# A decoder layer in split float32: gate and up products by seven products of sums, x updated by copies and adding DMAs

## The chip, the core and the metric

The kernel runs on one core of a Trainium2 chip. The metric is the time of one launch on the device in microseconds. The program is one long stream of instructions on five engines: TensorE (PE) multiplies, VectorE (DVE) and ScalarE (ACT) prepare operands and read the accumulators, GpSimd (POOL) does small jobs and issues some DMAs, and SyncE (SP) issues the weight loads.

## The reference

One layer on 256 rows of 2048 numbers, all in float32. The part that the change touches is the two half-step feed-forward networks, one at the start and one near the end:

```
x <- x + 1/2 * SwiGLU(RMSNorm(x)),  SwiGLU(h) = (silu(h @ w_gate) * (h @ w_up)) @ w_down
w_gate, w_up: 2048 x 5632      w_down: 5632 x 2048
```

Between the two stand a combined input projection, eight heads of latent attention, sixteen heads of a recurrent (RWKV-7) mixer, and an output projection; after the second comes a gated addition of a per-layer embedding.

## The kernel before, in words

**Split products.** Every operand of a large product is split in two float32r parts, hi and lo (value minus hi), and a product is three matmuls: hi by hi, hi by lo, lo by hi. Weights come as blocks of 1 MB, 128 partitions by 2048 numbers: four k-tiles (128 rows each) by 512 columns. A block goes through four steps. SP loads it to `raw` (3 buffers, `load_block`, which waits until DVE has split the block three before); ACT copies it to `whi` (3 buffers, `split_hi`, line 341); DVE subtracts to get `wlo` (2 buffers, `split_lo`, line 350); PE makes 24 matmuls of 128 by 128 by 512 from it (`products`, lines 364 to 366: four k-tiles, two tiles of 128 tokens, three matmuls). `split_lo` of a block can start when PE has finished the block two before, that is, when PE begins the block just before its own.

**The feed-forward network.** The 5632 hidden columns are taken in 11 groups of 512 (NFF = 11). Per group there are four blocks of gate, four of up and four of down (each of these four covers 512 columns of x). The first gate and up are made ahead; then ten passes follow (`pe_columns`, a loop of nine and one written out), each with the gate of group i+1, the transposition of h of group i (`h_turn`, eight transposes), the up of group i+1 and the down of group i. At the end of the network comes the down of the last group. Of one pass PE has 12 blocks of 24 matmuls and eight transposes.

**Banks of PSUM.** Gate uses banks 0 and 1, up 2 and 3, down 4 to 7 in turn, and h is transposed into 6 and 7. ACT applies silu to the gate sums (`silu`) while PE does up; DVE multiplies up by it (`hidden`) while PE does down; DVE adds each quarter of down to x in SBUF with two instructions of 128 by 512 (`update_x`, line 556).

**Start of a network.** x is transposed by PE (`turn_x`) and split by ACT and DVE into `xT_hi` and `xT_lo` (16 k-tiles of 256 tokens), two k-tiles a unit, while the first blocks are multiplied. ACT squares x (`square_x`, line 410) for the norm; DVE and POOL turn the sums into the factor `rstd`, which is first needed by silu. h of the first group is not transposed until the four blocks of gate of the next group are done, so PE has 21.8 us of other work in between.

**What sets the order.** The order on each engine is written out by hand: the semaphores `lo_ready`, `hi_ready` and `block_used` count blocks over the whole program. The queues are strict: where DVE waits, all later work of DVE waits.

Of the kernel before, what the change touches and what calls it, by code (L numbers as in the profile page):

```python
# [56 lines left out]
BLOCKS = GATE + 16  # L57

# [59 lines left out]
def hybrid_layer(nc, table, w, out):  # L118
    where = constant_table()[1]
    ctx = ExitStack()  # L120
    with ctx:
# [150 lines left out]
        def sem(name):  # L272
# [13 lines left out]
            sem, ("silu_ready", "h_ready", "h_turned", "hT_hi_ready", "hT_ready"))  # L286
        vec, pool_chain, zero_row = sem("vec"), sem("pool_chain"), sem("zero_row")
# [36 lines left out]
        READ_FFN1, READ_OUT, READ_FFN2 = 2, 2 + 4 * NFF, 6 + 4 * NFF  # L324
# [8 lines left out]

        def split_hi(act, n, it=0):
            if n >= BLOCKS:
                return
            wd = block_width(n)
            act.wait_ge(raw_loaded[n % RAW], 16 * (n // RAW + 1) + 64 * it)
            if n >= WHI:
                act.wait_ge(block_used, n - WHI + 1 + 12 * it)  # L340
            nc.scalar.activation(whi[:, n % WHI, 0:wd], raw[:, n % RAW, 0:wd], ACT.Copy).then_inc(hi_ready, 1)  # L341

        def split_lo(dve, n, it=0):
            if n >= BLOCKS:
                return
            wd = block_width(n)
            dve.wait_ge(hi_ready, n + 1 + 12 * it)
            if n >= WLO:
                dve.wait_ge(block_used, n - WLO + 1 + 12 * it)
            nc.vector.tensor_tensor(wlo[:, n % WLO, 0:wd], raw[:, n % RAW, 0:wd], f32(whi[:, n % WHI, 0:wd]),  # L350
                                    ALU.subtract).then_inc(lo_ready, 1)

# [17 lines left out]
        def turn_bank(k, u):  # L370

            return 4 + u if k == 2 and u < 2 else 2 + (u % 6 if k == 0 else u % 2)

        def turn_x(pe, k, units):

            for u in units:
                if k == 0 and u % 2 == 0:
                    pe.wait_ge(x_loaded[u // 2], 16)
                if k and u % 2 == 0:
                    pe.wait_ge(banks_read, (READ_FFN1 + 4 * NFF, READ_FFN2, READ_FFN2 + 4 * NFF)[k - 1] - 3 + u // 2)  # L380
                if u >= {0: 6, 2: 4}.get(k, 2):
                    pe.wait_ge(xT_ready, 8 * k + u - (1 if k else 5))
# [32 lines left out]
        def h_turn(pe, f, i, it=0, b=6):  # L415
            pe.wait_ge(h_ready, NFF * f + i + 1 + it)
            if b == 6:
                pe.wait_ge(banks_read, (READ_FFN1, READ_FFN2)[f] + 4 * i + 4 * it)
# [6 lines left out]
        def down(pe, f, n, i, it=0, last=False, turn_next=False):  # L425
            h_hi, h_lo = (last_hT_hi, last_hT_lo) if last else (hT_hi, hT_lo)
            for j in range(4):
                if turn_next and j == 2:
                    h_turn(pe, f, i + 1, b=0)
                if j == 0:  # L430
                    pe.wait_ge(hT_ready, NFF * f + i + 1 + it)
                if j >= 2 or last:
                    pe.wait_ge(banks_read, (READ_FFN1, READ_FFN2)[f] + 4 * i + j - 1 + 4 * it)
                products(pe, n + j, h_hi, h_lo, range(FKT), [(4 + 2 * (j % 2), 5 + 2 * (j % 2))], COLS, True, True, it)
# [3 lines left out]
        def first_products(pe):  # L438

            for j in range(FKT):  # L440
                pe.wait_ge(first_lo_ready if j < FKT // 2 else lo_ready, 1)
                for t in range(TT):
                    acc, c = PS[:, t, :], slice(j * COLS, (j + 1) * COLS)
                    a, b = xT_hi[:, j, t * P:(t + 1) * P], xT_lo[:, j, t * P:(t + 1) * P]
                    nc.tensor.matmul(acc, a, whi[:, 0, c], start=j == 0, stop=False)
                    nc.tensor.matmul(acc, a, wlo[:, 0, c], start=False, stop=False)
                    ins = nc.tensor.matmul(acc, b, whi[:, 0, c], start=False, stop=False)
            ins.then_inc(block_used, 1)

        def pe_columns(pe, f, n, i, it=0, turn_next=False):  # L450

            pe.wait_ge(silu_ready, NFF * f + i + 1 + it)
            for s in range(4):
                products(pe, n + s, xT_hi, xT_lo, range(4 * s, 4 * s + 4), [(0, 1)], COLS, s == 0, s == 3, it)
            h_turn(pe, f, i, it)
            for s in range(4):
                products(pe, n + 4 + s, xT_hi, xT_lo, range(4 * s, 4 * s + 4), [(2, 3)], COLS, s == 0, s == 3, it)
            down(pe, f, n + 8, i, it, turn_next=turn_next)

        def pe_ffn(pe, f, B):  # L460
            turn_x(pe, 2 * f, range(2 * f, 4))
            for s in range(4):
                pe.wait_ge(xT_ready, 16 * f + 2 * s + 2)
                if (f, s) == (0, 0):
                    first_products(pe)
                else:
                    products(pe, B + s, xT_hi, xT_lo, range(4 * s, 4 * s + 4), [(0, 1)], COLS, s == 0, s == 3)
                if s < 2:
                    turn_x(pe, 2 * f, (2 * s + 4, 2 * s + 5))
            if f == 0:  # L470
                pe.wait_ge(banks_read, 1)
                pe.wait_ge(xT_ready, 6)
                pe.wait_ge(gains_loaded, 80)
                nc.tensor.transpose(PS[:, 7, 0:70], gain_rows[:, :], ident[0:70, 0:70]).then_inc(gains_turned, 1)
            for s in range(4):
# [1595 lines left out]
```

## Time and profile before

| what | value |
|---|---|
| time, median of 3 runs | 2046.76 us (2046.42 to 2051.57) |
| profiled execution: span | 2045.4 us |
| PE busy | 2017.3 us, 99% |
| DVE busy | 1142.9 us, 56% |
| ACT busy | 869.0 us, 42% |
| POOL busy | 134.9 us, 7% |
| DMA, mean rate | 183 GB/s |

The span runs from the first to the last instruction of the profiled execution. The time of a run also has what lies around it: the lowest of the three runs is 1.0 us above the span, the median 1.4 us. The busy time of an engine is a sum over its instructions; a matmul shows 389 ns although one starts every 227 ns, since they overlap.

### The profile page before, as it was taken

How to read it: one execution, taken by the hardware profiler on the slowest of the kernel's cores; microseconds unless marked ns; L12 is line 12 of the kernel's file. 1: busy time of each engine (PE TensorE's matmuls, PEld its weight loads, DVE VectorE, ACT ScalarE, POOL GpSimd, SP SyncE). 2: the span in 40 equal slices, each digit the busy share in tenths (PEclk: the TensorE clock that was granted, in tenths of full speed). 3: DMA queues.
4: the chain of work that ended last, by engine and by line, in shares of the span. 5: the costliest groups of instructions: out<-in, count | busy, mean ns of one | idle time of the engine just before them, and what ended most of it. 6: DMA issues, size and time to landing. Idle time of an engine off the chain costs nothing.

```text
span 2045.4 us, 27608 instructions
## 1 busy us (share of the span) xinstructions
PE 2017.3 (99%) x11416; PEld 1683.9 (82%) x11416; DVE 1142.9 (56%) x1012; ACT 869.0 (42%) x847; POOL 134.9 (7%) x110
## 2 busy tenths in 40 slices
PE   8999999999999999999998999999999999999999
PEld 6888888888888889888787888888888888888887
DVE  4455545554555464756788545545554555545564
ACT  6333333333333345854344345333333333343353
POOL 0000000000000001344433000000000000000000
PEclk9999999999999999999999999999999999999999
DMA  7565555655655556667412556555656655555554
GB/s 262 186 195 195 185 185 191 198 185 187 195 193 185 191 155 215 201 196 221 123 41 70 190 165 206 185 186 194 193 185 190 195 189 187 193 195 185 186 185 144
DMA packets 190049, 373.62 MB, mean 183 GB/s; under 512 B 7110, under 2 KB 16962, under 8 KB 189980
## 3 DMA queue, kind: packets, MB, share of 16 engines
q1 hardware_dynamic: 186300, 361.47, 54.9%
q0 software_dynamic: 3680, 11.15, 1.8%
q8 instruction: 53, 0.87, 0.2%
q14 instruction: 16, 0.13, 0.0%
HBM read 363.94 MB, written 5.52 MB: 181 GB/s over the span
## 4 chain that ended last, share of the span: by engine, by line
PE 96%; DVE 2%; issue 0%; DMA 0%; ACT 0%; SPq 0%; DVEq 0%
PE PS L364 29%; PE PS L366 29%; PE PS L365 29%; PE PS L1341 3%; PE PS L421 1%; PE PS L385 1%; PE PS L1305 0%; DMA x_resid<-in_x 0%; DVE wlo L350 0%; DVE AB L1675 0%; PE PS L1412 0%; PE PS L1323 0%; PE PS L1279 0%; DVE AK L1675 0%; PE PS L1270 0%
## 5 line engine op out<-in xcount | busy, mean ns | idle before, releaser
L350 DVE TENSOR_TENSOR wlo<-raw,whi 128x2048 fp32r<-128x2048 f32 (+1 forms) x338 | 777.5, 2301 | 759.5 <-PE PS L366 755.5
L341 ACT ACTIVATE whi<-raw 128x2048 fp32r<-128x2048 f32 (+1 forms) x338 | 643.1, 1903 | 988.9 <-PE PS L366 983.9
L364 PE MATMUL PS<-whi,xT_hi 128*128 128x512 f32 (+2 forms) x1936 | 752.6, 389 | 0.0
L366 PE MATMUL PS<-whi,xT_lo 128*128 128x512 f32 (+2 forms) x1936 | 748.0, 386 | 0.0
L365 PE MATMUL PS<-wlo,xT_hi 128*128 128x512 f32 (+2 forms) x1936 | 747.5, 386 | 0.0
L366 PEld LDWEIGHTS PS<-whi,xT_lo 128*128 128x128 f32 x1936 | 363.5, 188 | 73.4
L364 PEld LDWEIGHTS PS<-whi,xT_hi 128*128 128x128 f32 x1936 | 363.6, 188 | 72.1 <-issue 0.4
L365 PEld LDWEIGHTS PS<-wlo,xT_hi 128*128 128x128 f32 x1936 | 363.7, 188 | 71.7
L364 PE MATMUL PS<-whi,hT_hi 128*128 128x512 f32 x680 | 264.8, 389 | 0.1
L366 PE MATMUL PS<-whi,hT_lo 128*128 128x512 f32 x680 | 264.6, 389 | 0.0
L365 PE MATMUL PS<-wlo,hT_hi 128*128 128x512 f32 x680 | 264.6, 389 | 0.0
L364 PEld LDWEIGHTS PS<-whi,hT_hi 128*128 128x128 f32 x680 | 127.6, 188 | 26.8 <-issue 0.5
L366 PEld LDWEIGHTS PS<-whi,hT_lo 128*128 128x128 f32 x680 | 127.6, 188 | 26.5
L365 PEld LDWEIGHTS PS<-wlo,hT_hi 128*128 128x128 f32 x680 | 127.6, 188 | 26.4
L556 DVE SCALAR_TENSOR_TENSOR x_resid<-PS,x_resid 128x512 f32<-128x512 f32 x184 | 118.0, 682 | 51.0 <-PE PS L366 51.0
L826 POOL TENSOR_TENSOR rstd<-rstd,con 128x2 f32<-128x2 f32 x6 | 6.3, 1044 | 1610.6 <-DVE rstd L821 1610.6
L403 DVE SCALAR_TENSOR_TENSOR xT_lo<-PS,gains,xT_hi 128x256 fp32r<-128x256 f32 x64 | 26.6, 477 | 28.1 <-ACT xT_hi L394 28.0
L394 ACT ACTIVATE xT_hi<-PS,gains 128x256 fp32r<-128x256 f32 x64 | 25.3, 476 | 38.0 <-PE PS L385 33.6
L1341 PE MATMUL PS<-XT,AB 64*64 64x64 f32 x640 | 26.4, 227 | 7.5 <-DVE XT L1689 4.8
L1341 PEld LDWEIGHTS PS<-XT,AB 64*64 64x64 f32 x640 | 22.1, 139 | 12.0 <-DVE XT L1702 5.7
L541 DVE SCALAR_TENSOR_TENSOR h<-PS,rstd,silu_g 128x512 f32<-128x512 f32 x44 | 30.9, 743 | 0.0
L547 DVE TENSOR_TENSOR hT_lo<-PS,hT_hi 128x1024 fp32r<-128x1024 f32 x20 | 24.5, 1224 | 10.1 <-ACT hT_hi L490 10.1
(334 smaller groups left out, 1079.6 us busy)
## 6 DMA issues: line engine op xcount, KB each, us to landing
raw<-in_w_gate SPq DMA_DIRECT2D x88, 1024.0 KB, 5.2
raw<-in_w_up SPq DMA_DIRECT2D x88, 1024.0 KB, 5.2
raw<-in_w_down SPq DMA_DIRECT2D x88, 1024.0 KB, 5.1
raw<-in_w_in SPq DMA_DIRECT2D x28, 1024.0 KB, 5.6
raw<-in_w_out SPq DMA_DIRECT2D x16, 1024.0 KB, 5.1
raw<-in_w_ple_gate SPq DMA_DIRECT2D x16, 1024.0 KB, 5.1
raw<-in_w_q_b SPq DMA_DIRECT2D x3, 1024.0 KB, 5.5
z_scratch<-zst POOLq DMA_DIRECT2D x6, 512.0 KB, 3.2
```

The lines of the kernel that those rows point to most:

```text
L341: nc.scalar.activation(whi[:, n % WHI, 0:wd], raw[:, n % RAW, 0:wd], ACT.Copy).then_inc(hi_ready, 1)
L350: nc.vector.tensor_tensor(wlo[:, n % WLO, 0:wd], raw[:, n % RAW, 0:wd], f32(whi[:, n % WHI, 0:wd]), ALU.subtract).then_inc(lo_ready, 1)
L364: nc.tensor.matmul(acc, a, whi[:, n % WHI, c], start=st, stop=False)
L365: nc.tensor.matmul(acc, a, wlo[:, n % WLO, c], start=False, stop=False)
L366: ins = nc.tensor.matmul(acc, b, whi[:, n % WHI, c], start=False, stop=en)
L385: ins = nc.tensor.transpose(PS[:, turn_bank(k, u), j * SEQ + t * P:j * SEQ + (t + 1) * P], x[:, t, (2 * u + j) * P:(2 * u + j + 1) * P], i ...
L394: ins = nc.scalar.activation(xT_hi[:, kt, :], PS[:, turn_bank(k, u), j * SEQ:(j + 1) * SEQ], ACT.Copy, scale=gains[:, 16 * k + kt:16 * k + ...
L403: ins = nc.vector.scalar_tensor_tensor(xT_lo[:, kt, :], PS[:, turn_bank(k, u), j * SEQ:(j + 1) * SEQ], gains[:, 16 * k + kt:16 * k + kt + ...
L541: ins = nc.vector.scalar_tensor_tensor(h[:, t, :], PS[:, 2 + t, :], rstd[:, 4 * f + t:4 * f + t + 1], silu_g[:, t, :], ALU.mult, ALU.mult)
L547: nc.vector.tensor_tensor((dst or hT_lo)[:, :, :].rearrange("p (b j) s -> p b (j s)", b=2), PS[:, b:b + 2, :], f32((hi or hT_hi)[:, :, :]) ...
L556: ins = nc.vector.scalar_tensor_tensor(x[:, t, j * COLS:(j + 1) * COLS], PS[:, b + t, :], factor, x[:, t, j * COLS:(j + 1) * COLS], ALU.mu ...
L1341: ins = nc.tensor.matmul(PS[half(c), bank, out_col:out_col + CHUNK], a[half(c), s, a_cols], b[half(c)], start=start, stop=stop)
```

## The change

**Seven products.** In the ten passes a unit of weights is no longer four k-tiles of gate or of up. It is two k-tiles of up and of gate side by side (`load_unit`, two DMAs of 512 KB), so a unit feeds four outputs: gate and up of both token tiles. Eight units make a pass. Four of them (even places) are multiplied as before, 24 matmuls. In the other four (odd places) the 2 by 2 block product (two token tiles by two k-tiles, two k-tiles by up and gate) is made as seven products of sums, 21 matmuls. This needs four sums of weights per unit (`weight_forms`: three dependent DVE instructions into `T`, split by ACT into `t_hi` and by DVE into `t_lo`, one buffer each), seven sums of x for each of four pairs of k-tiles (made once per network, `token_sums`, `token_hi`, `token_lo`), and seven accumulators in place of four, which DVE and ACT combine after the last unit (`first_sum`; `combine_gate`, one addition of 1024 and two of 512 numbers a partition; `combine_up`, two of 1024; each step but `combine_up`'s first waits for the one before).

**Order of a pass.** A pass is now: transposition of h of group i, eight units of gate and up of group i+1, four blocks of down of group i. For the first group PE makes eight units, all with 24 matmuls; the token sums are made in the last four of them, in place, and PE waits for the last (`tok_lo`) before the first pass, which begins with the transposition of that group's h.

**x.** In the passes DVE no longer adds down to x. ACT copies each quarter (two banks, 1024 numbers a partition, scaled by 0.5) to `xs` (two buffers), and POOL issues a DMA of 512 KB that adds it to x (`down_out`, `pool_add_x`). The last group of a network still goes by `update_x`, now one instruction, and DVE waits for all adding DMAs before it splits the second of the last four blocks. All eight banks change their use: down j goes to banks 2j and 2j+1, the seven products and the four outputs to banks 0 to 7.

```diff
-            for s in range(4):
-                products(pe, n + s, xT_hi, xT_lo, range(4 * s, 4 * s + 4), [(0, 1)], COLS, s == 0, s == 3, it)
+            if i:
+                pe.wait_ge(x_evac, evacs(f, i - 1, 2) + 4 * it)
             h_turn(pe, f, i, it)
-            for s in range(4):
-                products(pe, n + 4 + s, xT_hi, xT_lo, range(4 * s, 4 * s + 4), [(2, 3)], COLS, s == 0, s == 3, it)
-            down(pe, f, n + 8, i, it, turn_next=turn_next)
+            pe_units(pe, f, i, it)
+            down(pe, f, i, it, turn_next=turn_next)
...
+                for out in (OUT_11, OUT_21, OUT_12, OUT_22):
...
+                        if (f, s) == (1, 0) and out == OUT_21:
+                            pe.wait_ge(proj_evac, 2)
...
+            pe.wait_ge(tok_lo, SEVEN * f + SEVEN)
+            pe.wait_ge(banks_read, 2)
+            pe_pass(pe, f, 0)
...
+        def pe_units(pe, f, i, it):
+            n = FFN_BASE[f] + PAIRS + 12 * i
+            for v in range(PAIRS):
+                m = n + v
+                pe.wait_ge(lo_ready, m + 1 + 12 * it)
+                if v % 2 == 0:
...
+                    ins.then_inc(block_used, 1)
+                    continue
+                first, last = v == 1, v == 7
+                ins = seven_product(m, P1, False, first, last)
+                if last:
+                    ins.then_inc(p_done, 1)
+                seven_product(m, P3, False, False, last)
+                seven_product(m, P2, False, False, last)
+                pe.wait_ge(t_lo_ready, forms_of(m, it))
...
+                for product in (P6, P7, P4):
+                    ins = seven_product(m, product, True, first and product != P4, last)
+                    if last:
+                        ins.then_inc(p_done, 1)
+                seven_product(m, P5, True, first, last).then_inc(block_used, 1)
...
+                    pe.wait_ge(combined, steps(f, i, (1, 2, 4, 5)[j]) + 5 * it)
+                    banks = (2 * j, 2 * j + 1)
...
+        def weight_forms(dve, n, it=0):
+            src = raw[:, n % RAW, :].rearrange("p (k c) -> p k c", k=4)
...
+            nc.vector.tensor_tensor(T[:, 0:2, :], src[:, 1:3, :], src[:, 0:1, :].broadcast_to([P, 2, COLS]),
+                                    ALU.subtract).then_inc(t_pair, 1)
+            dve.wait_ge(t_pair, forms_of(n, it))
+            nc.vector.tensor_tensor(T[:, 2, :], T[:, 1, :], src[:, 1, :], ALU.add).then_inc(t_third, 1)
+            dve.wait_ge(t_third, forms_of(n, it))
+            nc.vector.tensor_tensor(T[:, 3, :], T[:, 2, :], src[:, 3, :], ALU.subtract).then_inc(t_ready, 1)
...
+        def combine_gate(dve, f, i, it):
+            done = 4 * ((NFF - 1) * f + i)
+            dve.wait_ge(s1_ready, (NFF - 1) * f + i + 1 + it)
+            dve.wait_ge(p_done, done + 2 + 4 * it)
+            nc.vector.tensor_tensor(G[:, 0:2, :], PS[:, 1:3, :], s1[:, :].unsqueeze(1).broadcast_to([P, 2, COLS]),
+                                    ALU.add).then_inc(combined, 1)
...
+        def combine_up(dve, f, i, it):
+            dve.wait_ge(block_used, FFN_BASE[f] + PAIRS + 12 * i + PAIRS + 12 * it)
...
...
+        def dve_pass(dve, f, i, it=0, turn_next=False):
+            n = FFN_BASE[f] + PAIRS + 12 * i
+            for s in range(12):
+                if s == 8:
+                    combine_up(dve, f, i, it)
+                split_lo(dve, n + s + 1, it)
+                if s == 0:
+                    hT_part_lo(dve, f, i, it)
+                if s in (0, 2, 4, 6):
+                    forms_lo(dve, n + s + 1, it)
+                if s in (1, 3, 5) or (s == 11 and not turn_next):
+                    weight_forms(dve, n + s + 2, it)
+                if s == 7:
+                    combine_gate(dve, f, i, it)
+                if s == 8:
+                    hidden(dve, f, i, it)
...
+            for s in range(PAIRS):
+                split_lo(dve, B + s + 1)
+                if s + 2 < PAIRS:
+                    xT_parts_lo(dve, 2 * f, (s + 2,))
+                if s >= 4:
+                    token_sums(dve, f, s - 4)
+                    token_lo(dve, f, s - 4)
...
+            weight_forms(dve, B + PAIRS + 1)
+            first_hidden(dve, f, B)
+            dve_pass(dve, f, 0)
+            with dve.Fori(0, NFF - 3) as it:
+                dve_pass(dve, f, 1, it)
+            dve_pass(dve, f, NFF - 2, turn_next=True)
+            for k in range(2):
+                dve.wait_ge(x_added[k], 32 * (NFF - 1) * (f + 1))
...
             for s in range(PAIRS):
+                if s + 2 < PAIRS:
+                    xT_parts_hi(act, 2 * f, (s + 2,))
+                split_hi(act, B + s + 2)
+                if s == 5:
                     square_x(act, 2 * f)
+                if s >= 4:
+                    token_hi(act, f, s - 4)
+            act.wait_ge(rstd_ready, 4 * f + 1)
+            first_silu(act, f, B)
...
+        def down_out(act, f, i, j, it=0):
+            act.wait_ge(block_used, FFN_BASE[f] + PAIRS + 12 * i + PAIRS + j + 1 + 12 * it)
...
+                act.wait_ge(x_added[j % 2], 16 * adds + 32 * it)
+            nc.scalar.activation(xs[:, j % 2, :, :], PS[:, 2 * j:2 * j + 2, :], ACT.Copy, scale=0.5).then_inc(x_evac, 1)
...
+        def pool_add_x(pool, f):
...
+                    pool.wait_ge(x_evac, evacs(f, i, j))
...
+                    pool.dma_start(x[:, :, j * COLS:(j + 1) * COLS], xs[:, j % 2, :, :], accum_op=ALU.add).then_inc(
+                        x_added[j % 2], 16)
```

`token_sums` is six DVE instructions, one of 512 numbers a partition and five of 128, with three waits on results of its own; `token_hi` is two ACT copies (512 and 384), `token_lo` two DVE subtractions of those sizes. `token_sums` of pair p+1 stands behind `token_lo` of pair p. In the odd units `split_hi` and `split_lo` take 1536 columns in place of 2048. At the very start x's first quarter is transposed alone before the first unit, where two quarters were.

## Rows read from the trace of the kernel before

**Rows 1.** The page: busy time (share of the span) and instructions of the engines.
```profile
PE 2017.3 (99%) x11416; PEld 1683.9 (82%) x11416; DVE 1142.9 (56%) x1012; ACT 869.0 (42%) x847; POOL 134.9 (7%) x110
```
**Rows 2.** The page: chain that ended last, shares by engine.
```profile
PE 96%; DVE 2%; issue 0%; DMA 0%; ACT 0%; SPq 0%; DVEq 0%
```
**Rows 3.** Timeline of PE, first matmuls of two blocks: start us, us, engine, line.
```profile
236.41 0.39 PE L364 MATMUL PS<-whi,hT_hi 128*128 128x512 f32 x1
...
241.85 0.39 PE L364 MATMUL PS<-whi,hT_hi 128*128 128x512 f32 x1
```
**Rows 4.** Timeline of DVE within one pass; in brackets the idle time before.
```profile
192.19 1.29 DVE L556 SCALAR_TENSOR_TENSOR x_resid<-PS,x_resid 128x512 f32<-128x512 f32 x2 [1.88 <-PE PS L366]
...
216.81 1.23 DVE L547 TENSOR_TENSOR hT_lo<-PS,hT_hi 128x1024 fp32r<-128x1024 f32 x1 [0.50 <-ACT hT_hi L490]
...
236.68 2.29 DVE L350 TENSOR_TENSOR wlo<-raw,whi 128x2048 fp32r<-128x2048 f32 x1 [3.15 <-PE PS L366]
238.89 1.41 DVE L541 SCALAR_TENSOR_TENSOR h<-PS,rstd,silu_g 128x512 f32<-128x512 f32 x2
...
258.37 1.29 DVE L556 SCALAR_TENSOR_TENSOR x_resid<-PS,x_resid 128x512 f32<-128x512 f32 x2 [1.88 <-PE PS L366]
```
**Rows 5.** Groups of DVE by form: busy us, mean ns, idle before.
```profile
L350 DVE TENSOR_TENSOR wlo<-raw,whi 128x1024 fp32r<-128x1024 f32 x4 | 4.9, 1226 | 7.6 <-PE PS L366 7.6
...
L1742 DVE SCALAR_TENSOR_TENSOR S<-PS,pc,SP 128x64 f32<-128x64 f32 x16 | 3.8, 280 | 1.2 <-PE PS L1430 1.1
...
L1610 DVE TENSOR_TENSOR kk<-kk,hsf 128x512 f32<-128x512 f32 x3 | 2.1, 692 | 0.1
...
L1059 DVE TENSOR_TENSOR sc<-PS,con 128x512 f32<-128x512 f32 x2 | 1.4, 680 | 0.0
```
**Rows 6.** Timeline of ACT at the start of the first network and in a pass.
```profile
26.32 1.57 ACT L394 ACTIVATE xT_hi<-PS,gains 128x256 fp32r<-128x256 f32 x4 [2.97 <-PE PS L385]
...
31.37 1.92 ACT L410 ACTIVATE scratch<-x_resid 128x2048 f32<-128x2048 f32 x1
...
35.45 1.92 ACT L341 ACTIVATE whi<-raw 128x2048 fp32r<-128x2048 f32 x1
...
39.89 1.28 ACT L485 ACT_TABLE_LOAD   x1
41.19 1.27 ACT L485 ACTIVATE silu_g<-PS,rstd 128x512 f32<-128x512 f32 x2
...
83.41 1.01 ACT L490 ACTIVATE hT_hi<-PS 128x1024 fp32r<-128x1024 f32 x1
```
**Rows 7.** Timeline of PE and ACT where the second network begins.
```profile
1219.03 1.04 PE L385 MATMUL PS<-con,x_resid 128*128 128x128 f32 x8
1219.82 0.47 PE L364 MATMUL PS<-whi,xT_hi 128*128 128x512 f32 x1
...
1219.23 2.07 ACT L1976 ACTIVATE proj<-PS 128x512 f32<-128x512 f32 x4 [1.61 <-PE PS L366]
```
**Rows 8.** DMAs from SBUF to SBUF issued by POOL: issue ns, then us to landing (min/median/max).
```profile
L1090 POOL DMA_DIRECT2D pvst<-zst x6: 547/551/562, 856.5 to 995.8; - x6
...
DMA to landing us min/median/max: 3.9/4.7/9.4
```
**Rows 9.** The page: DMA queue of the weights, packets, MB, share; and one of its issues.
```profile
q1 hardware_dynamic: 186300, 361.47, 54.9%
...
raw<-in_w_gate SPq DMA_DIRECT2D x88, 1024.0 KB, 5.2
```
**Rows 10.** Timeline of PE at the very start of the program.
```profile
10.73 1.97 PE L385 MATMUL PS<-con,x_resid 128*128 128x128 f32 x8 [2.15 <-DMA x_resid<-in_x]
12.35 0.78 PE L445 MATMUL PS<-whi,xT_hi 128*128 128x512 f32 x1
...
15.43 0.40 PE L446 MATMUL PS<-wlo,xT_hi 128*128 128x512 f32 x1
15.66 0.40 PE L447 MATMUL PS<-whi,xT_lo 128*128 128x512 f32 x1
```
**Rows 11.** Windows around it: us, busy per engine, PEclk, DMA share, GB/s.
```profile
12.00:16.00 4.00, 4.00 (x14) 3.29 (x13) 3.08 (x6) 3.36 (x5) 0.00 (x0) 1.00 1.05 387
```

More of the change, by code:

```diff
@@ L423, in h_turn, with evacs, steps, eight_products @@
             ins.then_inc(h_turned, 1)
-        def down(pe, f, n, i, it=0, last=False, turn_next=False):
+        def evacs(f, i, j):
+            return 4 * ((NFF - 1) * f + i) + j + 1
+        def steps(f, i, k):
+            return 5 * ((NFF - 1) * f + i) + k
+        OUT_11, OUT_21, OUT_12, OUT_22 = (1, 0, 1), (4, 1, 1), (6, 0, 0), (7, 1, 0)
+        def eight_products(n, out, kk, first, last):
+            bank, t, side = out
+            kt, c = 2 * pair_of(n) + kk, slice((2 * kk + side) * COLS, (2 * kk + side + 1) * COLS)
+            a, b = xT_hi[:, kt, t * P:(t + 1) * P], xT_lo[:, kt, t * P:(t + 1) * P]
+            nc.tensor.matmul(PS[:, bank, :], a, whi[:, n % WHI, c], start=first, stop=False)
+            nc.tensor.matmul(PS[:, bank, :], a, wlo[:, n % WLO, c], start=False, stop=False)
+            return nc.tensor.matmul(PS[:, bank, :], b, whi[:, n % WHI, c], start=False, stop=last)
@@ new lines, in hybrid_layer, with token_form, seven_product @@
+        P1, P2, P3, P4, P5, P6, P7 = (0, 0, 1), (1, 1, 3), (6, 6, 2), (4, 2, 3), (5, 3, 0), (2, 4, 2), (3, 5, 1)
+        def token_form(f, p):
+            if f < 4:
+                return tuple(a[:, 2 * p + f // 2, (f % 2) * P:(f % 2 + 1) * P] for a in (xT_hi, xT_lo))
+            return tuple(a[:, p, (f - 4) * P:(f - 3) * P] for a in (more_hi, more_lo))
+        def seven_product(n, product, of_sums, first, last):
+            bank, f, k = product
+            a, b = token_form(f, pair_of(n))
+            c = slice(k * COLS, (k + 1) * COLS)
+            hi, lo = (t_hi[:, k, :], t_lo[:, k, :]) if of_sums else (whi[:, n % WHI, c], wlo[:, n % WLO, c])
+            nc.tensor.matmul(PS[:, bank, :], a, hi, start=first, stop=False)
+            nc.tensor.matmul(PS[:, bank, :], a, lo, start=False, stop=False)
+            return nc.tensor.matmul(PS[:, bank, :], b, hi, start=False, stop=last)
@@ L426, in down @@
+        def down(pe, f, i, it=0, last=False, turn_next=False):
+            n = FFN_BASE[f] + PAIRS + 12 * i + (0 if last else PAIRS)
             h_hi, h_lo = (last_hT_hi, last_hT_lo) if last else (hT_hi, hT_lo)
@@ L466, in pe_ffn @@
                 else:
[L467 to L475, printed above, removed]
-                products(pe, B + 4 + s, xT_hi, xT_lo, range(4 * s, 4 * s + 4), [(2, 3)], COLS, s == 0, s == 3)
```

382 lines of the change are left out of this document (251 added, 131 removed).

## The prediction

> **What bounds the kernel now.** I read the page's busy shares first: PE is at work for 2017.3 of 2045.4 us, DVE and ACT about half of it [rows 1]. The chain that ended last agrees: 96% of the span are steps of PE [rows 2]. So a matmul taken out of the feed-forward networks is worth its own time, if nothing else comes to stand in front of PE. Next the pace: two neighbouring blocks begin their first matmuls 5.44 us apart [rows 3], 24 matmuls, so 0.2267 us each; the 0.39 us shown for one is overlap. The same point of two passes lies 66.18 us apart (192.19 to 258.37, [rows 4]): 12 x 5.44 = 65.28, and 0.90 for the eight transposes. DVE stands idle 3.15 us in front of a 2048-column subtraction of weights [rows 4], because that waits for PE; this slack is what the change spends.
>
> **The gain.** Four units of a pass take 21 matmuls for 24. Two networks of ten passes: 20 x 12 x 0.2267 = 54.4 us less on PE. Blocks of down, first groups and last groups keep their counts.
>
> **Inside a pass: is DVE quick enough?** Its durations: 2.29 us for 2048 columns, 2.21 to the next start (236.68 to 238.89, [rows 4]); 1.23 for 1024, 0.69 for 512 from SBUF and 0.68 from PSUM, 0.28 for a small one [rows 4, 5]; 1.76 for 1536, between 1.23 and 2.29; some 0.06 to hand one result to the next. DVE starts 0.27 after PE's new block (236.41 to 236.68, [rows 3, 4]). In an odd unit (21 x 0.2267 = 4.76 us) DVE does `split_lo` of the next unit (0.27 to 2.48) and `weight_forms` (1.23 + 0.69 + 0.69 and two hand-overs, to 5.20). In the even unit that follows (5.44 us), counted from its own start: ACT splits the sums from 0.5 to 2.4 (1.92, [rows 6]), DVE does `split_lo` of 1536 columns by then too (to 2.1), then `forms_lo`, 2.45 to 4.75. PE wants these sums nine matmuls into the next odd unit, at 5.44 + 2.04. So DVE is busy some nine tenths of a pair of units, and PE waits for none of it. The start of a pass holds too: `hT_lo` needs the transposes (0.9 + 0.2), ACT's copy of x first (1.0) and its copy of h (1.0, [rows 6]), so it ends near 3.5 and `forms_lo` near 6.4, while the unit in work ends at 6.34 and its sums are wanted at 8.4.
>
> **The combination behind the last unit.** Count from the start of that odd unit. The fourth product ends at 12 x 0.2267 + 0.17 = 2.89. DVE: 1024 from 2.98 to 4.22, 512 to 4.97, 512 to 5.71; `combine_up` overlaps a little, 1.23 to 6.86 and, after a hand-over, to 8.15; only then comes `split_lo` for the second block of down, to 10.36. PE has begun the first block of down at 4.76 and is done at 10.20. With the hand-over PE waits 0.25 us each pass: 5.0 us in all. Bounds: nothing, if two steps overlap more than shown, and 1.4 us a pass (28 us in all), if each of the six steps were 0.2 us longer. I take 0.25, since each step has a row of its form. Behind it there is 3 us of slack in every block of down.
>
> **The adding DMAs in the loop.** They take 4 x 0.68 x 2 = 5.4 us of DVE and put four copies of 1024 (1.0 each) on ACT, which has the room. A DMA may take long here: ACT wants a buffer back two blocks (10.9 us) later, and PE wants that bank only after a further one, so up to some 14 us cost nothing. DMAs from SBUF to SBUF landed in 3.9 to 9.4 us [rows 8]. Of the engines' share: 186300 packets of weights took 54.9% of 16 x 2045.4 us, 0.096 us each [rows 9]; a quarter of x is 256 packets, 1024 a pass, and even at twice that price they add 1024 x 0.19 / 16 = 12 us to the 37 us of weights in a pass of 64. The Trainium skill ("Collectives: The Full Stack", The bandwidth ceiling) says that a reducing transfer reaches half the rate of a copy because it reads two sources; no row here shows an adding DMA. By that rule the price is the doubled one just taken. Cost in the loop: 0. A weight load of 5.2 us [rows 9] starts when DVE has split the block three before, and has over 3 us to spare. The two loads of 512 KB in place of one of 1 MB have the same 2 KB rows: 0.
>
> **The start of a network, the step that costs most.** Before, h of the first group had 21.8 us of other work to hide behind; now PE stands still until it is there. Count from the start of unit 5 (of 0 to 7). A unit with its four transposes lasts 5.44 + 0.40 = 5.84 (eight delay the next block by 0.79, [rows 7]).
> `token_sums` is 0.69 + five of about 0.28 with three hand-overs, partly overlapped: 2.1 us. ACT's `token_hi` is 1.05 (0.63 for 512 as in silu, [rows 6]), `token_lo` 1.15, with hand-overs 4.4 for the round trip, in which DVE does nothing else.
> DVE: `xT_lo` to 1.85, round trip 0 to 6.25, `split_lo` of unit 6 to 8.5. PE: unit 5 ends at 5.84, waits 2.65.
> DVE: `xT_lo` to 9.25, sums 1 to 11.35; but ACT has the squares in front of `token_hi` (31.37 to 35.45, 4.08 us, [rows 6]), until 12.75; round trip ends 15.0, `split_lo` of unit 7 to 17.2. PE: unit 6 from 8.5 to 13.95, waits 3.3.
> DVE: round trip 2 to 21.55, `split_lo` to 23.95, round trip 3 to 28.3, `weight_forms` to 31.0 (silu, 1.27, and the 1.28 us table load of [rows 6] run on ACT beneath it), `first_hidden` 1.41 to 32.4. PE: unit 7 from 17.25 to 22.7, then idle 9.8.
> Sum 15.75 a network, 31.5 us. Bounds: at least the last gap with `weight_forms`, `first_hidden` and one round trip without lateness (8 us), at most 18 if each small DVE step costs twice the 0.28. I keep 15.75: the queue is strict and the rows are near.
>
> **PE after a long gap.** At the start of the program PE had been idle, and its work ran at half pace: eight transposes held the next matmul for 1.62 us (10.73 to 12.35, against 0.79), then seven matmuls took 3.08 (12.35 to 15.43, against 1.59), the next 0.23 [rows 7, 10]: 2.3 us lost. The matmuls' spacing of 0.43 us is that of 1.2 GHz, though the column of the granted clock says 1.00 there [rows 11]. No row shows PE idle for long later. Bounds: 0, and 2.3 for each of four gaps, 9. I take 2.3 for the two long gaps: 4.6 us.
> The Trainium skill ("TensorE: Matmul & The Clock Gate", The HAM clock gate) states that idleness throttles PE to half rate and that activity must release it. It speaks for the charge: without it the sum would be 4.6 better.
>
> **The end of a network.** DVE waits for the last adding DMA before it splits the second of the last blocks. From the end of down 3: copy 1.2 (with its hand-over), POOL's issue 0.55 within the landing time, landing 6 (between 4.7 and 9.4, [rows 8], as it reads twice), `split_lo` 2.3 and hand-overs 0.2: 9.75 against 5.44 of PE's work, 4.3 us a network, 8.6 in all. Bounds: a landing of 3.9 gives 2.2, one of 9.4 gives 7.7; 4.4 to 15.4 in all. The second network's second output waits for ACT's last copies of `proj` (1219.23 to 1221.3), six matmuls after 1219.0: 0.9 us [rows 7]. At the very start PE need not transpose two quarters at half pace before the first product: 1.0 us gained, by 0.5 to 1.5.
>
> **Sum.** 54.4 - 5.0 - 31.5 - 4.6 - 8.6 - 0.9 + 1.0 = 4.8 us less. The profiled span of 2045.4 becomes 2040.6; the runs' median stands 1.4 above the span, so 2046.8 becomes 2042.0.
>
> **The rivals.**
> *A, the starts hide better (28%).* If small DVE steps overlap more and PE keeps its pace, a start costs 10 us in place of 18: 2026. For it: five of six steps work on 128 columns only, whose price I have from a 64-column row. Against it: the squares on ACT are 4.08 us whatever DVE does.
> *B, nothing waits (6%).* 2046.8 - 54.4 + 0.9 - 1.0 = 1992. Against it stands `first_hidden`, which must be late.
> *C, slower: the combination (17%).* The six steps on DVE between the fourth product and the second block of down. Place: each pass. Price: beyond 0.25 us, 20 us for each further microsecond. At 1.3 us a pass it is 21 us more: 2063; it decides from 0.5 us a pass (even) and makes the kernel slower by over 0.3% from 0.8. For it: no idle time between the steps is planned, and POOL's descriptor work could stretch them. Against it: rows for each form.
> *D, slower: the adding DMAs (7%).* If one packet takes over 0.42 us (64 - 37 = 27 us for 1024 packets on 16 engines), the weights come late in every pass; at 0.5 us it is 32 us against 27, 5 us a pass, 2142. Against it: the highest landing time of [rows 8].
> That the change doesn't save the matmuls is excluded: they are issued one by one.
>
> **How the numbers follow.** My case has 42%, its own range 2034 to 2050. 0.3%, about what a measurement of this kernel tells from no change, is 6.1 us, so its 4.8 us falls mostly within. Faster: 17 of the 42, 25 of A's 28, B's 6: 48. Same: 23, 3 of A, 3 of C: 29. Slower: 2, 14 of C, 7 of D: 23. The range reaches from A's 2026 a little further, 2022, to C's 2063.
>
> **What would show it.** Right: PE with 240 fewer large matmuls; passes of 63.7 us (8 x 5.44 + 4 x 4.76 + 0.9 + 0.25); before the first `h_turn` of each network a PE gap of 8 to 11 us released by h, and two smaller ones before units 6 and 7; PE idle once per pass before the second down, under 0.5 us, released by `wlo`; a gap of 2 to 8 us before the second of the last blocks. Wrong: a gap before the first pass below 5 us, a pass above 64.5 us, matmuls waiting for loads of weights, or adding DMAs that land later than 14 us.

## Result and profile after: slower by 0.6%

The kernel after takes 2059.66 us, median of 4 runs (2057.96 to 2061.57); the kernel before, timed beside it, 2047.13 us (2046.42 to 2051.57). The ratio is 1.0060, 95% interval 1.0045 to 1.0074: slower. I had forecast 2042.0. The time lies inside my wide range, on the wrong side of no change.

The page after, the lines that answer to [rows 1, 2, 9]: busy time; shares of the chain; DMA queues (packets, MB, share); issues (KB, median us to landing).
```profile
PE 1993.9 (97%) x11176; PEld 1649.8 (80%) x11176; DVE 1507.0 (73%) x1324; ACT 1071.6 (52%) x1043; POOL 237.3 (12%) x190
...
q1 hardware_dynamic: 189116, 361.48, 51.8%
q0 software_dynamic: 25440, 53.09, 13.6%
...
PE 93%; DVE 4%; issue 1%; ACT 1%; DMA 1%; SPq 0%; DVEq 0%
...
raw<-in_w_gate SPq DMA_DIRECT2D x176, 512.0 KB, 4.9
...
x_resid<-xs POOLq DMA_DIRECT2D x80, 512.0 KB, 6.8
```
PE issues the 240 fewer large matmuls (11416 to 11176), yet its busy time fell by only 23.4 us of the 54.4 that they are worth: some matmuls became slower. The view of what PE waits for (us in all, times, longest) has three new rows:
```profile
PE PS L521 <- DVE h L753: 14.8, 2, 7.6
PE PS L540 <- DVE wlo L426: 10.9, 4, 3.1
PE PS L466 <- DVE wlo L426: 9.1, 2, 5.0
```
They are the start of a network (h late, and two units late) and its end. And the windows view (us, busy per engine, PEclk, DMA share, GB/s) shows a granted clock that before, at 0.999 over the whole span, dipped only once while PE had work, for 3.4 us:
```profile
60.00:63.40 3.40, 2.83 (x7) 2.28 (x8) 2.24 (x7) 1.02 (x3) 0.00 (x0) 0.52 0.53 143
70.20:80.40 10.20, 5.15 (x16) 4.42 (x17) 8.04 (x11) 5.42 (x6) 0.00 (x0) 0.51 0.36 118
262.50:326.50 64.00, 64.00 (x286) 52.50 (x285) 51.82 (x36) 34.84 (x24) 4.80 (x4) 1.00 0.75 229
729.00:735.80 6.80, 5.75 (x14) 4.53 (x15) 4.24 (x3) 0.00 (x0) 0.00 (x0) 0.51 0.70 210
...
1124.90:1131.70 6.80, 5.78 (x37) 4.70 (x37) 4.20 (x9) 2.45 (x3) 1.44 (x1) 0.51 0.01 2
```
A PEclk of 0.51 is the lower level, 1.2 GHz. Nine such stretches, 51 us together, stand in the profile after, some of them partly over time in which PE stood idle; in a pass (third row) the clock is full. The profiled execution is the longest of the four (2061.57 us).

The two profiled executions, cut at the transpositions of h, x and p (us; the gate blocks that stood ahead of the first transposition of h before, 21.76 a network, are counted with the passes). The column "forecast" has the terms of my sum.

| part | before | after | difference | forecast |
|---|---|---|---|---|
| network 1: start, to the first transposition of h | 59.6 | 75.3 | +15.6 | +14.8 |
| its passes and last group, to that of x | 679.3 | 668.7 | -10.5 | -18.1 |
| projections, mixer, to that of p | 429.8 | 435.4 | +5.6 | 0 |
| network 2: start | 96.7 | 112.9 | +16.3 | +16.7 |
| its passes and last group | 679.3 | 666.7 | -12.6 | -18.1 |
| rest | 100.8 | 100.8 | 0 | 0 |
| sum | | | +14.4 | -4.8 |

So the starts came as forecast. What is missing is 13.1 us inside the two networks and 5.6 us in a part that the change doesn't touch.

### The profile page after: what moved, and what is told of

Read it like the earlier page. It is cut to its first block, busy times and chain, and to the rows that moved or that the text cites. A ratio compares the mean times of both kernels' runs of the same rounds, so it can differ in the third digit from the quotient of the medians.

```text
span 2059.8 us, 28962 instructions
## 1 busy us (share of the span) xinstructions
PE 1993.9 (97%) x11176; PEld 1649.8 (80%) x11176; DVE 1507.0 (73%) x1324; ACT 1071.6 (52%) x1043; POOL 237.3 (12%) x190
## 3 DMA queue, kind: packets, MB, share of 16 engines
q0 software_dynamic: 25440, 53.09, 13.6%
## 4 chain that ended last, share of the span: by engine, by line
PE 93%; DVE 4%; issue 1%; ACT 1%; DMA 1%; SPq 0%; DVEq 0%
PE PS L466 14%; PE PS L468 14%; PE PS L467 14%; PE PS L540 8%; PE PS L542 8%; PE PS L541 8%; PE PS L558 6%; PE PS L557 6%; PE PS L559 6%; PE PS L1621 2%; PE PS L521 1%; DVE wlo L426 1%; PE PS L487 1%; DMA x_resid<-xs 1%; PE PS L1585 0%
## 5 line engine op out<-in xcount | busy, mean ns | idle before, releaser
L426 DVE TENSOR_TENSOR wlo<-raw,whi 128x2048 fp32r<-128x2048 f32 (+2 forms) x338 | 732.4, 2167 | 367.7 <-PE PS L468 265.3
L417 ACT ACTIVATE whi<-raw 128x2048 fp32r<-128x2048 f32 (+2 forms) x338 | 605.9, 1793 | 242.9 <-PE PS L468 152.6
L540 PE MATMUL PS<-whi,xT_hi 128*128 128x512 f32 x768 | 306.9, 400 | 15.0 <-DVE wlo L426 10.9
L542 PE MATMUL PS<-whi,xT_lo 128*128 128x512 f32 x768 | 303.1, 395 | 0.0
L541 PE MATMUL PS<-wlo,xT_hi 128*128 128x512 f32 x768 | 301.8, 393 | 0.0
L453 DVE TENSOR_TENSOR t_lo<-T,t_hi 128x2048 fp32r<-128x2048 f32 x80 | 183.4, 2293 | 32.8 <-ACT t_hi L448 32.8
L466 PE MATMUL PS<-whi,xT_hi 128*128 128x512 f32 (+2 forms) x536 | 206.3, 385 | 0.0
L468 PE MATMUL PS<-whi,xT_lo 128*128 128x512 f32 (+2 forms) x536 | 203.6, 380 | 0.0
L467 PE MATMUL PS<-wlo,xT_hi 128*128 128x512 f32 (+2 forms) x536 | 203.4, 379 | 0.0
L540 PEld LDWEIGHTS PS<-whi,xT_hi 128*128 128x128 f32 x768 | 146.3, 191 | 47.0 <-issue 15.7
L541 PEld LDWEIGHTS PS<-wlo,xT_hi 128*128 128x128 f32 x768 | 146.3, 190 | 31.0
L468 PEld LDWEIGHTS PS<-whi,xT_lo 128*128 128x128 f32 x536 | 101.1, 189 | 18.8
```

The lines of the kernel that those rows point to most:

```text
L417: nc.scalar.activation(whi[:, n % WHI, a:wd], raw[:, n % RAW, a:wd], ACT.Copy).then_inc(hi_ready, 1)
L426: nc.vector.tensor_tensor(wlo[:, n % WLO, a:wd], raw[:, n % RAW, a:wd], f32(whi[:, n % WHI, a:wd]), ALU.subtract).then_inc(lo_ready, 1)
L453: nc.vector.tensor_tensor(t_lo[:, :, :], T[:, :, :], f32(t_hi[:, :, :]), ALU.subtract).then_inc(t_lo_ready, 1)
L466: nc.tensor.matmul(acc, a, whi[:, n % WHI, c], start=st, stop=False)
L467: nc.tensor.matmul(acc, a, wlo[:, n % WLO, c], start=False, stop=False)
L468: ins = nc.tensor.matmul(acc, b, whi[:, n % WHI, c], start=False, stop=en)
```

## The experiments

All ratios are to the kernel before, timed on the same chip. My theory after the result: the seven products pay, and the loss is (a) the starts, (b) the end of each network, where the wait for the last adding DMA is charged at its own length and again at half clock, (c) a slightly slower pace of the matmuls, (d) lost time in the mixer.

**The wait at the end, alone.** DVE splits the second of the last blocks first and waits for the DMAs after it:
```
-            for k in range(2):
-                dve.wait_ge(x_added[k], 32 * (NFF - 1) * (f + 1))
             for s in range(4):
                 if s:
                     split_lo(dve, B + FFN_BLOCKS - 4 + s + 1)
+                    if s == 1:
+                        for k in range(2):
+                            dve.wait_ge(x_added[k], 32 * (NFF - 1) * (f + 1))
```


> The changed kernel, but at the end of each network VectorE waits for the adding DMAs only after it has split the second of the last four blocks, just before its first addition to x. Theory (the two ends of a network cost a gap of 5.0 and 4.1 us on TensorE and, after it, a stretch at half clock that costs some 3 us each): 2059.7 - 9.1 - 6.2 = 2044 us, gaps at the ends under 0.5 us, no half-clock stretch there. Rival 1 (the half clock there is not due to the gap): 2059.7 - 9.1 = 2051. Rival 2 (the adding DMA is late anyway, so the additions to x and the turning of x are late in its place): 2056 to 2060.

2045.31 us (10 runs), ratio 0.999 (0.998 to 0.9999). In the timeline after (start, duration, in brackets the idle time before):
```profile
719.56 1.03 ACT L689 ACTIVATE xs<-PS 128x1024 f32<-128x1024 f32 x1 [2.60 <-PE PS L468]
...
720.89 1.20 POOL L1374 DMA_DIRECT2D x_resid<-xs  x1 [4.24 <-ACT xs L689]
...
727.61 4.49 DVE L426 TENSOR_TENSOR wlo<-raw,whi 128x2048 fp32r<-128x2048 f32 x2 [11.12 <-DMA x_resid<-xs]
...
730.05 0.77 PE L466 MATMUL PS<-whi,last_hT_hi 128*128 128x512 f32 x1 [5.03 <-DVE wlo L426]
```
and with the wait moved:
```profile
724.34 2.29 DVE L426 TENSOR_TENSOR wlo<-raw,whi 128x2048 fp32r<-128x2048 f32 x1 [3.20 <-PE PS L468]
727.80 1.22 DVE L797 SCALAR_TENSOR_TENSOR x_resid<-PS,x_resid 128x1024 f32<-128x1024 f32 x1 [1.17 <-DMA x_resid<-xs]
```
PE no longer waits, and the last group up to x takes 28.28 us, as before (28.27), for 36.43 and 35.37 in the kernel after. So one moved wait is worth 14.4 us of the median. I had priced it at 8.6: the gap was right (5.0 and 4.1 us for 4.3), but with each one came a stretch of 6.8 us at half clock, which costs some 3 us more (15.3 us in all, less 9.1 for the gaps, is 6.2 for the two).

**x as before, by DVE.** No copies, no adding DMAs; DVE adds each quarter of down in the passes (`pass_update`, one instruction of 1024):
```
-                if s >= 9:
-                    down_out(act, f, i, s - 9, it)
...
+                if s >= 9:
+                    pass_update(dve, f, i, s - 9, it)
...
-            for k in range(2):
-                dve.wait_ge(x_added[k], 32 * (NFF - 1) * (f + 1))
```


> The changed kernel, but in the passes VectorE adds down to x as one instruction of 1024 numbers, reading PSUM; no ScalarE copies and no adding DMAs. Theory (VectorE has about 3 us of slack in each block of down, the DMAs buy nothing): passes stay at 64.0 us, the end gaps go, total as in the run with the late wait, 2044 +- 3. Rival (the DMAs are there since VectorE has no time): it is 5 us more of VectorE's work a pass and the sums of weights come late; passes of 65 to 69 us, total 2060 or more. If the copies and DMAs also slow TensorE's pace (0.2267 us a matmul before, 0.228 to 0.229 in the gate and up units now), passes fall to 63.5 and the total to 2034.

2043.49 us (10 runs), 0.9982 (0.9972 to 0.9991). A loop pass lasts 64.03 us as in the kernel after. So in the loop the adding DMAs neither cost nor give anything, and the slower pace isn't theirs.

**The gaps filled.** The same waits, but PE makes useless matmuls in them (30 before the first pass, 20 in the last group), so that it isn't idle:
```
+            keep_busy(pe, 2, 30)
             pe.wait_ge(tok_lo, SEVEN * f + SEVEN)
...
                 products(pe, n + j, h_hi, h_lo, range(FKT), [banks], COLS, True, True, it)
+                if last and j == 0:
+                    keep_busy(pe, 0, 20)
```


> The changed kernel with useless matmuls of 512 columns on TensorE in its long gaps: 30 before the first h is transposed, 20 before the second of the last four blocks, in each network, into banks that are free. They take 6.8 and 4.5 us, less than the gaps, so they should delay nothing. Theory (half clock after a gap is a cost of its own, about 2.6 and 1.8 us after the first gaps and 3.1 after each end gap): 2059.7 - 10.6 = 2049, no half-clock stretch behind them. Rival (the stretches are chance or don't cost, since other engines set the pace there): 2059 to 2060.

2050.17 us (10 runs), 1.0011 (1.0001 to 1.0021): 9.5 us off the kernel after for work that does nothing. This isolates what half clock costs. The clock where the first pass begins, and the transposition there:
```profile
68.00:80.40 12.40, 11.76 (x57) 9.57 (x56) 9.93 (x15) 7.52 (x8) 0.00 (x0) 1.00 0.44 137
```
```profile
75.38 1.06 PE L521 MATMUL PS<-con,h 128*128 128x128 f32 x8 [0.64 <-DVE h L761]
```
The kernel after has 1.94 us for these eight transposes at PEclk 0.51, and starts them at nearly the same time (75.25). The first passes fall from 66.71 and 65.80 us to 64.13, the last groups from 36.43 and 35.37 to 32.91 and 33.36.

**The new order with eight products only.** The units, the order of a pass and the adding DMAs stay, but odd units are multiplied with 24 matmuls; the sums of weights and of x and the combination are left out, with their waits (of this the cut shows the first line).
```
-            return (k - PAIRS) % 12 in (1, 3, 5, 7)
+            return False
```


> The changed kernel without the seven products: all units of gate and up by 24 matmuls, no sums of weights or x, no combination; silu and up read PSUM directly. Kept: the units with gate and up side by side, h of a group transposed at the start of a pass, x by ScalarE copies and adding DMAs. Theory: passes of 66.2 us as before the change, so 2.1 us a pass more than with seven products; the first gap shrinks to some 4.1 us (table load, silu, h), the ends cost 4.5 + 3.1 each: 2047 + 2 x (4.1 + 2.3) + 2 x 7.6 = 2075. So seven products are worth 2075 - 2060 = 15 us net. Rival (seven products cost nothing but what they save, their sums are hidden): 2060 + 54 = 2114.

2080.27 us, 1.0159 (1.0142 to 1.0176), 20.6 us above the kernel after. So the seven products are worth 20.6 us net of what their sums cost at the starts. A loop pass lasts 66.19 us, exactly as before, so order and layout are free in the loop; 64.03 is 2.16 less, and twenty passes give 43 us, of which the token sums take back 10.4 and 10.6 us at the starts (75.3 to 64.9, 112.9 to 102.3).

**The starts, spread.** Token sums go with units 1, 2, 4 and 6 in place of 4 to 7; the squares on ACT thereby stand behind the third of them; `first_hidden` goes ahead of `weight_forms`; silu's table is loaded early.
```
-                if s >= 4:
-                    token_sums(dve, f, s - 4)
-                    token_lo(dve, f, s - 4)
+                if s in (1, 2, 4, 6):
+                    token_sums(dve, f, (1, 2, 4, 6).index(s))
+                    token_lo(dve, f, (1, 2, 4, 6).index(s))
...
-            weight_forms(dve, B + PAIRS + 1)
             first_hidden(dve, f, B)
+            weight_forms(dve, B + PAIRS + 1)
```


> The changed kernel with its first group reordered: the sums of x for pairs 0 to 3 stand behind units 1, 2, 4 and 6 and ahead of the split of the x units (VectorE was idle there), ScalarE's squares behind unit 5's x, the table for silu is loaded ahead, and h of the first group comes before the sums of weights. Theory (the start of a network costs 13 to 14 us of gaps and 2 to 3 us of half clock, all from VectorE's queue): the gaps before units 6 and 7 go (2.4 and 3.0), the long one falls from 7.6 to 3.2 us, and the half clock after it mostly goes: 2059.7 - 2 x 9.8 - 4.4 = 2036 us. Rival (the work is only moved: VectorE is simply full there): gaps of the same sum at other units, 2055 to 2060.

2039.03 us (2034.55 to 2043.45), 0.9955 (0.9938 to 0.9971). The starts take 65.4 and 102.5 us for 75.3 and 112.9; the gaps before units 6 and 7 are gone, the long one is half:
```profile
65.41 1.94 PE L521 MATMUL PS<-con,h 128*128 128x128 f32 x8 [3.38 <-DVE h L756]
```
(7.57 in the kernel after.) My walk along DVE's queue had named the right steps. The four runs spread over 9 us: the two with a mean granted clock of 0.995 took 2034.55 and 2036.51 us, those with 0.991 and 0.992 took 2041.56 and 2043.45.

**All repairs together.** Both kernels have the spread starts, and `split_lo` of the second block of down ahead of `combine_up`; the one called best_dma keeps the adding DMAs with the moved wait, best_dve adds on DVE.
```
+                split_lo(dve, n + s + 1, it)
                 if s == 8:
                     combine_up(dve, f, i, it)
-                split_lo(dve, n + s + 1, it)
```


> The same with x by ScalarE copies and adding DMAs and the late wait. Theory: 2045.3 - 28.6 = 2017, 1 to 3 us above the version with x by VectorE. Rival (with VectorE fuller at the starts, the adding DMAs pay): equal or below it.

> x added by VectorE in the passes, the reordered first group, and the split of the second block of down ahead of the last two combining steps (which takes away 0.23 us a pass). Theory, gains adding up: 2043.5 (x by VectorE) - 24 - 20 x 0.23 = 2015 us. Rival (gains overlap, the gaps share a cause): 2025 to 2035.

best_dma: 2018.10 us (2015.88 to 2020.51), 0.9856 (0.984 to 0.9873). best_dve: 2021.05 us, 0.9868 (0.9852 to 0.9885), 6 us over its expectation. A loop pass falls from 64.03 to 63.87 us in both, by the combination's wait. best_dma beats both given kernels, by 1.4% and 2.0%; between the two of them the intervals overlap.

**The mixer.** It is the same code, yet took 3.4 to 9.6 us more in the profile of each kernel above. In its timeline PE stands still once for 1.1 to 1.6 us with "issue" as the reason, waiting for nothing that the profile shows. My guess, which no view can show directly, was that instructions come late in long straight code, so I wrote out one pass of the kernel before on PE, which lengthens PE's program and changes nothing else:
```
-            with pe.Fori(0, NFF - 2) as it:
-                pe_columns(pe, f, B + 8, 0, it)
+            pe_columns(pe, f, B + 8, 0)
+            with pe.Fori(0, NFF - 3) as it:
+                pe_columns(pe, f, B + 20, 1, it)
```


> The kernel before, but TensorE's first pass of each network is written out in front of the loop, as the change does, so that its instructions lie elsewhere in later code; nothing else differs. In every kernel with the change so far the mixer between the networks takes 433.5 to 435.4 us from the first turn of x after network 1 to the turn of p (before: 429.8), with a TensorE gap of 1.4 to 2.0 us that no engine releases and a half-clock stretch behind it. Theory (where refills of TensorE's instructions fall sets this): the same 4 to 5 us appear here, 2051 us. Rival (something else of the change, such as engine or memory state): 429.8 us in the mixer, 2047 us.

2048.70 us, 1.0009 (0.9999 to 1.0019): between the two expectations; the mixer took 431.1 us for 429.8, with an "issue" wait of 1.1 us that the kernel before has not. It settled nothing, so I put 64, 128 and 192 waits that are already satisfied into best_dma, on PE between the first network and the mixer:
```
+            for _ in range(64):
+                pe.wait_ge(ident_loaded, 16)
             pe_w_in(pe)
```


> best_dma with 64 waits that are already satisfied added to TensorE's stream between the first network and the mixer (a few ns each, under 1 us together). In best_dma the unchanged mixer takes 437.3 us from the transposition of x to that of p, in the kernel before 429.8. Theory (TensorE's instructions arrive late at a place of the long straight code, and where that falls depends on how many instructions stand ahead): the mixer changes by 3 us or more in at least one of the three paddings (64, 128, 192), and its place of lost time moves; with 64 the median is 2011 to 2018. Rival (something else, such as an engine that comes later or the placement of data): the mixer stays at 436 to 439 us in all three, median 2018.5.

> As the run with 64, with 128 satisfied waits. Theory: the mixer's time differs from that of the other paddings by 3 us or more in at least one of them. Rival: 436 to 439 us as without padding, median 2019.

> As the run with 64, with 192 satisfied waits. Theory: the mixer's time differs from that of the other paddings by 3 us or more in at least one of them. Rival: 436 to 439 us as without padding, median 2019.

| kernel | median us | mixer, profiled | its "issue" waits of PE |
|---|---|---|---|
| best_dma | 2018.10 | 437.3 | 0.53 and 1.35 |
| with 64 | 2017.65 | 431.7 | 1.11 and 0.59 |
| with 128 | 2025.38 | 439.3 | 5.08 and 1.4 |
| with 192 | 2027.98 | 440.9 | 8.59 and 1.8 |

The ratios of the padded three are 0.9857, 0.9895 and 0.9909, each within 0.0017. The place of the "issue" wait moves with the number of instructions ahead. Without padding:
```profile
1104.01 0.37 PE L1696 MATMUL PS<-S,W1T 64*64 64x64 f32 x3 [1.35 <-issue]
```
with 64:
```profile
1035.32 0.33 PE L1625 MATMUL PS<-vv,AK 64*64 64x64 f32 x3 [1.11 <-issue]
```
The padding isn't free, as I had expected (a few ns a wait). The third 64 waits cost 3.5 us of standing still, 55 ns each, right behind the network:
```profile
739.42 1.94 PE L487 MATMUL PS<-con,x_resid 128*128 128x128 f32 x8 [8.59 <-issue]
```
The first 64 are hidden, since PE has a wait of 1.50 us for DVE at that place anyway. Of the mixer's time in the table, 3.6 and 7.1 us in the last two rows are the padding's own (from the second transposition of x to the third 6.12 and 9.63 us, for 2.53 in best_dma); without them 435.7 and 433.8 are left.

The other half is the clock. The same wait of 2.24 us for `XT` was followed by matmuls at half pace in best_dma (1.78 us for 32) and not with 64 waits (1.15 us):
```profile
980.36 1.78 PE L1625 MATMUL PS<-XT,AB 64*64 64x64 f32 x32 [2.24 <-DVE XT L1973]
```
```profile
978.38 1.15 PE L1625 MATMUL PS<-XT,AB 64*64 64x64 f32 x32 [2.24 <-DVE XT L1973]
```
The windows view of the first of these executions has 0.52 there, that of the second 1.00:
```profile
980.50:983.90 3.40, 3.40 (x70) 3.40 (x70) 1.71 (x6) 0.74 (x3) 0.00 (x0) 0.52 0.98 258
```
```profile
980.50:983.90 3.40, 3.08 (x84) 2.64 (x80) 3.30 (x11) 0.55 (x2) 1.08 (x1) 1.00 0.78 222
```
Half-clock stretches in the mixer add up to 3.4 us before, 13.6 after, 17.0 in best_dma and 6.8 with 64 waits. Half of the 10.2 us by which after exceeds before, and its "issue" wait of 1.6, make 6.7 for 5.6 measured. But with 64 waits the median is that of best_dma, though one profile is 5.9 us shorter. So two things are shown: where PE stands still without a releaser depends on the number of instructions ahead, and short waits are followed by half clock in some executions and not in others. That instructions come late there is inferred, and how much of the 5.6 us is steady stays open.

**The pace.** After, a pair of units takes 10.30 us where 45 matmuls at 0.2267 make 10.20. Is it the sums' load on DVE and ACT? From the second pass on the sums were made over 64 columns in place of 512, so t_hi and t_lo keep old values; PE's matmuls are the same.
```
+            c = form_cols(n)
...
-            nc.vector.tensor_tensor(T[:, 2, :], T[:, 1, :], src[:, 1, :], ALU.add).then_inc(t_third, 1)
+            nc.vector.tensor_tensor(T[:, 2, 0:c], T[:, 1, 0:c], src[:, 1, 0:c], ALU.add).then_inc(t_third, 1)
```


> The kernel after, in which from the second pass of each network on the sums of weights and their two splits are made over 64 columns in place of 512, so that the rest of T, t_hi and t_lo keeps the first pass's values (a part of the computation is left out); TensorE's matmuls are the same. A loop pass lasts 64.03 us, 0.33 more than 12 units at 0.2267 us a matmul with their waits. Theory (the added work of DVE and ACT slows TensorE's matmuls a little, 0.2284 to 0.2294 us in place of 0.2267): the pass falls to 63.7 us, median 2053.5. Rival (the pace goes with the 21-matmul units themselves): the pass stays at 64.0, median 2059.5.

2058.78 us, 1.006 (1.0043 to 1.0077), loop pass 64.04: as the rival expected. The load went (`t_lo` by form: 419 ns in place of 2293), the pace stayed.
```profile
L457 DVE TENSOR_TENSOR t_lo<-T,t_hi 128x256 fp32r<-128x256 f32 x72 | 30.1, 419 | 0.0
```
Matmul starts in the kernel after show where it sits; in the last products of an odd unit they lie 0.23 and 0.24 apart for 0.2267, at the same places in every pair:
```profile
343.90 0.40 PE L557 MATMUL PS<-t_hi,xT_hi 128*128 128x512 f32 x1
344.14 0.39 PE L558 MATMUL PS<-t_lo,xT_hi 128*128 128x512 f32 x1
344.37 0.40 PE L559 MATMUL PS<-t_hi,xT_lo 128*128 128x512 f32 x1
344.61 0.39 PE L557 MATMUL PS<-t_hi,xT_hi 128*128 128x512 f32 x1
```
So do most of the first ten matmuls of the unit or block behind it, which read `whi` and `wlo` as before. In the kernel with eight products, and in the kernel before, only the first six of a pass do so. So the slower pace goes with PE's own stream of an odd unit, its mid-unit waits or the order of its operands, and lasts a little beyond it; which of them, no run tells.

## Why the prediction was wrong, step by step

- **What bounds the kernel, the 240 matmuls, 54.4 us:** right. PE is still the chain, and the matmuls are gone.
- **DVE quick enough in a pass:** right. No wait for `wlo`, `t_lo` or the transposed h in a loop pass.
- **The combination, 0.25 us a pass:** right, 0.16 to 0.22. Down takes 21.98 us where four blocks make 21.76, and the moved `split_lo` gave 0.16 back. The six steps, from [rows 4, 5], ran as walked:
```profile
310.33 1.23 DVE L762 TENSOR_TENSOR G<-PS,s 128x1024 f32<-128x1024 f32 x1 [0.44 <-PE PS L559]
...
314.18 1.23 DVE L777 TENSOR_TENSOR h<-PS,h 128x1024 f32<-128x1024 f32 x1
315.31 2.28 DVE L426 TENSOR_TENSOR wlo<-raw,whi 128x2048 fp32r<-128x2048 f32 x1
```
  Rival C had its place right and no price.
- **The adding DMAs cost nothing in the loop:** right. They landed in 5.6 to 9.8 us, median 6.8, where I took 6; about 14 were free. (The 3.9 and 9.4 of [rows 8] are the landings of single rows copied to the same tile, which that view puts together with the six large DMAs; those took 4.1 to 6.4, median 4.6.) Their queue's share rose from 1.8% (3680 packets) to 13.6%: 3890 of the 16 engines' us for 21760 packets, 0.18 us each, where I had priced 0.19. The rule of the Trainium skill ("Collectives: The Full Stack", The bandwidth ceiling), half the rate of a copy, fits that against the 0.096 of [rows 9]. Rival D is out.
- **The starts, 15.75 us each:** the sum right (31.9 with the small terms, for 31.4), the parts less so:
```profile
51.76 0.47 PE L540 MATMUL PS<-whi,xT_hi 128*128 128x512 f32 x1 [2.41 <-DVE wlo L426]
...
60.57 0.77 PE L540 MATMUL PS<-whi,xT_hi 128*128 128x512 f32 x1 [3.03 <-DVE wlo L426]
...
75.25 1.94 PE L521 MATMUL PS<-con,h 128*128 128x128 f32 x8 [7.57 <-DVE h L753]
```
  DVE walked from the `split_lo` of unit 7 to h in 14.9 us (60.34 to 75.25) for 15.2 forecast. But the 3.03 us gap, for which I had charged no clock, went with half clock (0.77 for a matmul), so unit 7 took 7.0 us for 5.44, under cover of DVE: the last gap is shorter by as much as PE was slower. Three gaps of 13.0 and 1.5 of slow matmuls leave 1.1 of the 15.6, where I had forecast a gain of 1.0 at the very start. The first product does begin earlier, at 11.66 us for 12.35; a part of what is left is that a unit with four transposes lasts 5.93 us for 5.84 forecast, and the rest isn't broken down. Rivals A and B are out.
- **Half pace after the long gaps, 4.6 us:** right, 2.7 and 1.8 in the first passes. (The 1.00 of [rows 11] was no contradiction: the clock records in the trace before begin only at 15.35 us, just where the matmuls' spacing falls from 0.43 to 0.23 us, and the view puts 1.00 where there is no record.)
- **The end of a network, 8.6 us: this step failed.** I asked "is PE idle long enough to lose its clock?" of the 9.8 us gap and not of the 4.3 us one, though "no row shows PE idle for long later" held for both. It measured 15.3: 9.1 of gaps, for my 8.6, and 6.2 of slow matmuls, a term that I had put at nothing without a reason. What I had cited on the clock gate ("TensorE: Matmul & The Clock Gate", The HAM clock gate, in the Trainium skill: idleness throttles, activity releases) gives no ground to charge the long gap alone, and the trace agrees: a PEclk of 0.51 or 0.52 with the gaps of 3.0, 4.1 and 5.0 us. The miss is 6.7 us.
- **The pace: missed.** I multiplied 21 by a spacing read from blocks whose operands are always the same two buffers. A pass measured 64.03 for 63.7: 6.5 us over the twenty.
- **"Nothing else moves": missed.** The mixer's 5.6 us; of the 12.5 by which the medians differ it may be less, as said.

The sum of the misses, 6.7 + 6.5 + 5.6, is 18.8 of the 19.2 us between -4.8 and +14.4. Each alone would have turned my 4.8 us of gain into a loss of 1 to 2 us, and without any one of them the kernel would still be slower; my case's own range, 8 us above its middle, had room for only one of them.

## What to carry to other kernels

Before spending an engine's idle time, list every new gap of the bound engine, short ones too, and charge each with its length and again with the half-clock stretch that goes with it (some 3 us each for gaps of 4 to 5 us here; for shorter gaps it is a matter of chance). Work that does nothing, put into the gap, may be cheaper than the gap. A wait for a slow transfer belongs behind whatever the bound engine needs next from the same queue: one moved line gave 0.7% here, more than the whole change lost. A change of this kind is worth judging only after its starts and ends are repaired: seven products of sums lost 0.6% as written and gain 1.4% with three local moves.

## What the runs showed of the hardware

- A gap of PE of 2.2 us was followed by half clock in one execution and not in another. Of the twelve gaps of 3.4 to 3.6 us ahead of the transposition of h (six profiles with the spread starts) eight went with a half-clock stretch of 3.4 or 6.8 us; gaps of 4 to 5 us at the ends of the networks did in every profile that had them, eight of eight. In one series the kernel before ran within 1.3 us over 13 runs; beside it best_dma, with more such gaps, within 4.6 us over 4.
- PE stood still for 1.1 to 1.8 us in the mixer of every kernel with the change, waiting for nothing that the profile shows, and in the kernel before for 0.2 us. A satisfied wait took PE 55 ns (3.5 us for 64), unless it was hidden behind another wait.
- An adding DMA of 512 KB from SBUF to SBUF, 256 rows of 2 KB, took 1.20 us of POOL's time to issue. The plain one of [rows 8], 0.55, had 127 rows of 4 KB, and a plain one of 256 rows of 2 KB to HBM (`z_scratch<-zst`) took 0.79, so at most the rest, 0.4 us, is the price of adding.
